# Seven block products of eight for the convolution's second-half projections in a hybrid gated block

## What is computed

```python
proj = jnp.einsum('bld,dn->bln', u, w_in)
(c_b, c_c, c_x, c_z, q, k, v, r, lr_f, lr_b, m_a, m_b) = jnp.split(proj, split_idx, axis=-1)
y_conv = c_b * short_conv_centred(c_c * c_x, conv_w) * jax.nn.silu(c_z)      # 3 taps
p_conv = jnp.einsum('blc,cd->bld', y_conv, w_out_c)
# ... gated linear attention in two directions gives o ...
p_gla = jnp.einsum('blc,cd->bld', rms_norm(o, gla_g) * jax.nn.silu(r), w_out_g)
merged = jax.nn.sigmoid(m_a) * p_conv + jax.nn.sigmoid(m_b) * p_gla
out = jnp.einsum('bld,de->ble', merged, w_out)
return h + rms_norm(out, g_post)
```

## Time and profile before

| | |
|---|---|
| median of 3 runs | 2919.62 us (2919.02 to 2920.57) |
| profiled execution | 2921.19 us |
| its span on the slowest core (core 3) | 2919.6 us |
| spans of the 8 cores | 2909.6 to 2919.6 us |
| granted clock of TensorE, mean of a core | 0.995 to 0.997 |
| PE busy | 2851.8 us, 98% |
| DVE, ACT, POOL busy | 1815.4, 1381.3, 831.7 us |

### The profile page before, as it was taken

One profiled execution on the slowest core, in us unless ns is written; L12 is line 12 of the kernel. 1 busy time (PEld: TensorE's weight loads), 2 busy tenths in 40 slices (PEclk: granted clock), 3 DMA queues, 4 the chain that ended last, 5 costly groups with the idle time before them and its releaser, 6 DMA issues.

```text
span 2919.6 us, 53947 instructions; the slowest of 8 cores (2909.6 to 2919.6 us)
## 1 busy us (share of the span) xinstructions
PE 2851.8 (98%) x16092; PEld 1468.0 (50%) x16092; DVE 1815.4 (62%) x2786; ACT 1381.3 (47%) x2567; POOL 831.7 (28%) x1278
## 2 busy tenths in 40 slices
PE   6999999999999999999999999999999999999998
PEld 3565644444456554444456555444445655544443
...
GB/s 183 134 140 116 125 101 183 232 173 113 197 106 77 75 84 115 110 232 127 111 216 81 75 68 89 123 142 230 97 152 170 78 72 71 84 137 127 118 112 140
DMA packets 340764, 373.44 MB, mean 128 GB/s; under 512 B 208112, under 2 KB 218352, under 8 KB 339968
## 3 DMA queue, kind: packets, MB, share of 16 engines
...
## 4 chain that ended last, share of the span: by engine, by line
PE 94%; DMA 2%; DVE 1%; issue 1%; POOL 1%; ACT 0%; SPq 0%; DVEq 0%; POOLq 0%; ACTq 0%
PE ps L479 94%; DMA sb_onT<-x 0%; DMA sb_onT<-sb_ON 0%; DMA wsc<-sb_W 0%; DMA sb_W<-w_all 0%; DMA sb_KT<-sb_GR 0%; POOL sb_stat L674 0%; PE ps L484 0%; POOL sb_SB L514 0%; DMA sb_ycT<-x 0%; DVE sb_CS L509 0%; DVE sb_ycT L505 0%; DVE sb_TB L509 0%; POOL sb_stat L514 0%; DVE sb_CS L505 0%
## 5 line engine op out<-in xcount | busy, mean ns | idle before, releaser
L479 PE MATMUL ps<-sb_uT,sb_W 128*128 128x512 bf16 (+2 forms) x7840 | 1625.9, 366 | 1.9 <-DMA sb_W<-w_all 1.2
L479 PEld LDWEIGHTS ps<-sb_uT,sb_W 128*128 128x128 bf16 (+1 forms) x7840 | 707.8, 98 | 808.9 <-issue 20.4
L496 ACT ACTIVATE sb_CS<-ps 128x512 f32<-128x512 f32 (+2 forms) x528 | 281.2, 540 | 636.2 <-PE ps L479 605.2
L505 DVE TENSOR_TENSOR sb_CS<-ps,sb_CS 128x512 f32<-128x512 f32 (+1 forms) x408 | 281.0, 691 | 187.9 <-PE ps L479 177.6
L509 DVE SCALAR_TENSOR_TENSOR sb_CS<-sb_CS,ps 128x512 f32<-128x512 f32 x256 | 175.8, 687 | 295.6 <-PE ps L479 284.3
L505 POOL TENSOR_TENSOR sb_GR<-sb_CS 128x512 bf16<-128x512 f32 x128 | 162.1, 1267 | 671.0 <-DVE sb_CS L509 658.5
L479 PE MATMUL ps<-sb_GR 128*128 128x512 bf16 (+2 forms) x1792 | 347.5, 318 | 1.1 <-POOL sb_GR L505 1.1
L505 POOL TENSOR_TENSOR sb_CS<-sb_CS 128x512 f32<-128x512 f32 x128 | 164.8, 1291 | 276.7 <-DVE sb_CS L509 168.6
L479 PE MATMUL ps<-sb_V,sb_uT 128*128 128x256 bf16 x2048 | 239.3, 274 | 0.0
L479 PE MATMUL ps<-sb_onT,sb_W 128*128 128x512 bf16 x1024 | 232.2, 379 | 2.6 <-DVE sb_onT L509 2.6
L509 DVE SCALAR_TENSOR_TENSOR sb_CS<-sb_CS,sb_convw 128x512 f32<-128x512 bf16 x256 | 209.8, 832 | 39.8 <-ACT sb_CS L496 27.6
...
## 6 DMA issues: line engine op xcount, KB each, us to landing
sb_W<-wsc SPq DMA_DIRECT2D x440, 256.0 KB, 2.6
sb_onT<-x SPq DMA_DIRECT2D x56, 512.0 KB, 5.4
sb_W<-wst SPq DMA_DIRECT2D x112, 256.0 KB, 2.8
sb_W<-w_all POOLq DMA_DIRECT2D x80, 256.0 KB, 6.2
sb_GR<-x SPq DMA_DIRECT2D x40, 512.0 KB, 5.5
wsc<-sb_W SPq DMA_DIRECT2D x80, 256.0 KB, 4.4
y<-sb_GR SPq DMA_DIRECT2D x32, 512.0 KB, 3.4
sb_ycT<-x SPq DMA_DIRECT2D x32, 512.0 KB, 5.4
```

The costliest lines, as they stand in the source:

```text
L479: S.add("pe", lambda e: e.matmul(out, lhsT=lhsT, rhs=rhs, start=start, stop=stop, skip_group_check=more), r, w, cost=max(0.025, free_n(rhs ...
L496: S.add("act", lambda e: e.activation(out=out, in_=in_, func=func, **kw), r, w, table=TABLE.get(func), cost=0.17 + 0.82e-3 * free_n(in_) + ...
L505: S.add(eng, lambda e: e.tensor_tensor(out=out, in0=a, in1=b, op=op), r, w, cost=ecost(eng, free_n(out), narrow(out, a, b)))
```

## The change

The convolution stage computes its four projections for each j as two groups of seven products, `(cc, cx)` and `(z, cb)`, in a new function `conv7`. `Seven` is rewritten: the result of p1 is copied by ACT, p6 is followed by a DVE sum that is written back into its PSUM bank, on which p7 and p4 then go on summing, and ACT copies that bank and p5's. The last product p4 of a group is put into the next group, after that one's p6; an output tile follows it in two of three groups. Weight sums for all 16 pairs of the convolution are made in batch 0, in the first half's blocks (`own`), where the weights are held until both of a pair are there. In the gate stages p7 and p4 move apart, with output projections between. Scratch regions `SB`, `SM`, `ON` become one region `OS` that also holds `Seven`'s copies. The next batch's token loads 2 to 7 (and 8 to 11 behind them) may be emitted only after the gate unit mb of block i - 2 of the second half; before, only the end of the first gates and the reuse of their four buffers held them. The diff, cut to its core:

```diff
-    wst_d = nc.dram_tensor("wst", [8 * 128 * 8, 256], BF16, kind="Internal").ap()
+    wst_d = nc.dram_tensor("wst", [24 * 128 * 8, 256], BF16, kind="Internal").ap()
...
+        def npk():
+            best = None
+            for i in range(8):
+                if i in G["held"]:
+                    continue
+                k = ("ps", i)
+                t = max([S.free["pe"]] + [S.last_w[k].end if k in S.last_w else 0.0] + [r.end for r in S.readers.get(k, ())])
+                t -= 0.0 if (i ^ 1) not in G["held"] else 0.4
+                if best is None or t < best[0]:
+                    best = (t, i)
+            if best is None:
+                raise NotReady()
+            i = best[1]
+            G["held"] = G["held"] + (i,)
+            return psb[i], [("ps", i)]
...
-        sd1, sd2, sd5 = (Buf("CS", 8192 + z * 2048, 2048) for z in range(3))
+        sdA = [Buf("CS", 8192 + z * 2048, 2048) for z in range(3)]
+        def sdL(dt):
+            return lrT[:, :].bitcast(dt), [("lr", 0), ("lr", 1)]
+        sdB = [Buf("OS", z * 2048, 2048) for z in range(3)]
+        sdC = [sdB[0], sdB[1], sdL]
+        wtmp = {"m": [Buf("CS", 8192, 2048), Buf("CS", 10240, 2048)], "c": [Buf("onT", 28 * KB + z * 2048, 2048) for z in range(2)]}
...
+        class Seven:
...
+            def __init__(self, pair, X, Y, t0, sd, done, total):
+                self.t0, self.sd, self.done, self.total = t0, sd, done, total
+                self.h = [w2.reserve(X), w2.reserve(("S", pair, 0)), w2.reserve(("S", pair, 1)), w2.reserve(("Y", Y))]
+                self.bk = {}
...
+            def keep(self, bk, z):
+                o_ap, o_k = self.sd[z](F32)
+                act(o_ap, bk[0][:, 0:512], AF.Copy, bk[1], o_k)
+            def bank(self, name, new=False):
+                if new:
+                    G["s7", self, name] = npk()
+                return G["s7", self, name]
+            def p1(self):
+                a = self.bank("a", True)
+                self.mul(a, 0, 0, self.u(0, 0), True)
+                self.keep(a, 0)
+            def p5(self):
+                e = self.bank("e", True)
+                self.mul(e, 1, 0, self.tt(0), True)
+                self.keep(e, 2)
+            def p6(self):
+                b_ = self.bank("b", True)
+                self.mul(b_, 1, 512, self.tt(1), True)
+                s_ap, s_k = self.sd[0](F32)
+                tt("dve", b_[0][:, 0:512], b_[0][:, 0:512], s_ap, ALU.add, b_[1] + s_k, b_[1])
+                self.keep(b_, 1)
+                rel(self.h[1])
+            def p2(self):
+                a = self.bank("a")
+                self.mul(a, 0, 512, self.u(4, 0), False)
+                rel(self.h[0])
+                self.done(0, 0, a)
+            def p3(self):
+                e = self.bank("e")
+                self.mul(e, 2, 0, self.u(4, 512), False)
+                self.total(0, e, self.sd[1])
+                drop(e[1])
+            def p7(self):
+                b_ = self.bank("b")
+                self.mul(b_, 2, 512, self.tt(2), False)
+                rel(self.h[2])
+                self.total(1, b_, self.sd[2])
+            def p4(self):
+                b_ = self.bank("b")
+                self.mul(b_, 3, 0, self.tt(3), False)
+                rel(self.h[3])
+                self.done(1, 0, b_)
...
+                    if own:
+                        sums_w(hs["cc"], hs["cx"], 8 + j, wtmp["c"])
+                        rel(hs["cc"])
...
+        def conv7(b, j):
...
+            def done1(f, s, bk):
+                if f == 0:
+                    o_ap, o_k = ccb[0](F32)
+                    act(o_ap, bk[0][:, 0:512], AF.Copy, bk[1], o_k)
+                else:
+                    times(pv(BF16, 1, 512), (bk[0][:, 0:512], bk[1]), ccb[0](F32), "dve")
+                drop(bk[1])
+            def total1(f, bk, part):
+                dst = ccb[1] if f == 0 else part
+                d, p_ = dst(F32), part(F32)
+                tt("dve", d[0], bk[0][:, 0:512], p_[0], ALU.add, bk[1] + p_[1], d[1])
+                if f == 1:
+                    times(pv(BF16, 513, 512), d, ccb[1](F32))
+            def done2(f, s, bk):
+                if f == 0:
+                    z_ap, z_k = szb[0](BF16)
+                    act(z_ap, bk[0][:, 0:512], AF.Silu, bk[1], z_k)
+                    drop(bk[1])
+                else:
+                    G["cb", me] = bk
+            def total2(f, bk, part):
+                d, p_ = part(F32), part(F32)
+                tt("dve", d[0], bk[0][:, 0:512], p_[0], ALU.add, bk[1] + p_[1], d[1])
+                if f == 0:
+                    z_ap, z_k = szb[1](BF16)
+                    act(z_ap, d[0], AF.Silu, d[1], z_k)
...
+            def cb(s):
+                out = ycT(1, j)(BF16, s * 512, 512)
+                if s:
+                    times(out, sdC[2](F32), tcb[1](F32))
+                else:
+                    bk = G.pop(("cb", me))
+                    times(out, (bk[0][:, 0:512], bk[1]), tcb[0](F32), "dve")
+                    drop(bk[1])
...
+            put("C", lambda: cb(1), ("cb", me, 1), [("sv", b, 1, j, "z", "p7")])
+            put("C", lambda: cb(0), ("cb", me, 0), [("sv", b, 1, j, "z", "p4")])
+            g1 = Seven(8 + j, ("cc", j), ("cx", j), 1024, sdB, done1, total1)
+            g2 = Seven(16 + j, ("z", j), ("cb", j), 1024, sdC, done2, total2)
+            u1 = g1.units((b, 1, j, "c"), {"p4": ("cx", me, 1)})
+            u2 = g2.units((b, 1, j, "z"), {"p2": ("z", me, 0), "p3": ("z", me, 1)})
+            if j > 2:
+                last = (b, 1, j - 1)
+                for p, a in (("p2", ("zm", last, 0)), ("p3", ("zm", last, 1)), ("p5", ("cb", last, 1))):
+                    u2[p][2].append(a)
+            return u1, u2
...
-                    sv = Seven((b, hh, d), d, ("ma", d), ("mb", d), t0, fin)
-                    for p, fn, ti in (("p1", sv.p1, None), ("p5", sv.p5, 0), ("p6", sv.p6, 1), ("p2", sv.p2, None), ("p3", sv.p3, None),
-                                      ("p7", sv.p7, 2), ("p4", sv.p4, 3)):
-                        units[p] = (fn, ("mb", b, hh, d, 1) if p == "p4" else ("sv", b, hh, d, p),
-                                    [("TT", b, hh, ti)] if ti is not None else [])
+                    sv = Seven(d, ("ma", d), ("mb", d), t0, sdB if hh else sdA, done, total)
+                    units.update(sv.units((b, hh, d), {"p4": ("mb", b, hh, d, 1)}))
+                    if hh and d == 0:
+                        units["p1"][2].extend([("cb", (b, 1, 7), 0), ("cb", (b, 1, 7), 1)])
                 ho = {n: w1.reserve((n, d)) for n in ("oc", "og")}
...
-                    order = ["p1", "p5", "p6", "p2", "p3", "p7", ("oc", 0), "p4", ("oc", 1), ("og", 0), ("og", 1)]
+                    order = ["p1", "p5", "p6", "p2", "p3", ("oc", 0), "p7", ("oc", 1), "p4", ("og", 0), ("og", 1)]
...
-                    a.append(("og", b - 1, 0, 7, 1))
+                    a.append(("mb", b - 1, 1, i - 2, 1) if 2 <= i < 8 else ("og", b - 1, 0, 7, 1))
...
+            pend = None
+            n = 0
-                ca, cz, cbb, _ = conv_units(b, 1, j)
-                units = ca + cz + cbb
-                for n, (fn, name, aft) in enumerate(units):
-                    if n % 4 == 0 and t7:
+                for g in conv7(b, j):
+                    for p in ("p1", "p5", "p6"):
+                        put("D2", *g[p])
+                    if pend is not None:
+                        put("D2", *pend["p4"])
+                    if n % 3 < 2 and t7:
                         put("D2", *t7.pop(0))
-                    put("D2", fn, name, aft)
+                    for p in ("p2", "p3", "p7"):
+                        put("D2", *g[p])
+                    pend = g
+                    n += 1
+            if t7:
+                put("D2", *t7.pop(0))
+            put("D2", *pend["p4"])
```

183 lines of the change are left out of this document (89 added, 94 removed).

## The result

The changed kernel takes 3026.11 us (median; the kernel before 2920.1 us in the same session): 1.036 times as long, 95% interval 1.034 to 1.038. The prediction was 2900 us with a range of 2880 to 2936 us: a gain was forecast, and the kernel became slower, by 90 us beyond the upper end of the range. The profiled execution took 3026.24 us with a span of 3024.7 us.

The account below looks back on a forecast made before the run. PE was taken as the bound, busy 2851.8 of 2919.6 us. Terms -41.4 - 2 + 17.6 + 4 + 2 = -19.8 us took 2921.19 to 2901.4, less 1.57 to 2899.8, stated as 2900 us, range 2880 to 2936.

Parts of the forecast that it names:

- What goes: Convolution stage: 192 matmuls fewer at 215.8 ns each, a gain of 41.4 us.
- pace: Rival: a removed matmul gives back only 118 ns, 22.6 us for the 192, ending at 2919 us; chance 0.03.
- Where cover is thin: Four convolution groups per batch without an output tile lose 1.1 us each through late VectorE or weights, 17.6 us.
- covered: Rival: loads stand ahead of stores and VectorE keeps up, leaving exit and 1 us of batch 0: 2881 us; chance 0.14.
- The price of a tap: VectorE in the convolution stage: each of four taps per channel block priced at 0.89 us.
- (b): Groups without a tile: weight load fits by 0.3 to 0.6 us; behind store and residual load PE waits 1.4 us.
- (a): p7 after p6 in groups without a tile: 0.7 us spare; a scale or two taps ahead cost 0.6 to 1.1 us.
- slower rival: Store and residual load precede weights in each thin group, VectorE's queue costs 0.9 us in all sixteen: 2936 us; chance 0.26.
- A wait on a free bank: Sign against the forecast: PE waiting on a free PSUM bank would show it wrong.
- Batch 0: First phase: weight sums for 16 pairs, 32 stores and longer-held buffers cost 2 us, bounds 0 and 18 us.
- The gate stages: Output projections between p3, p7 and p4 take back 2 us of PE's waits on VectorE sums (0 to 2.9).
- Exit: Last convolution group: p4 directly behind p7 with a VectorE sum between, 1.0 us per batch, 4 us.

Follow-up runs that it names:

- e12: Changed kernel with seven products only for (cc, cx), both z products ahead of p7, batch 0's second half as before, first-half residual sums on VectorE: ratio 0.9983 to kernel before.
- e5: Changed kernel with the residual sum of the first half's output tiles made by VectorE, never POOL: ratio 1.0245 to the kernel before.
- e11: e5 plus an output tile in each of the first eight groups, so groups without one come last: two runs, 2982.8 and 2988.5 us.
- e7: Changed kernel with the output tiles' stores issued from POOL's queue instead of SP's: ratio 1.0441 to the kernel before.
- e1: Changed kernel without the weight sums of batch 0's convolution pairs, their stores and the longer-held buffers: ratio 1.0279 to the kernel before.
- e13: Changed kernel with batch 0's 64 VectorE sums made from token tiles, not stored, no buffer held: ratio 1.0292 to the kernel before.
- e15: e11 with batch 0's second half as before the change, making the sums of its twelve pairs there: ratio 1.0051 to the kernel before.
- e2: Changed kernel with the old convolution stage and no convolution weight sums in batch 0: ratio 1.0003 to the kernel before.
- e4: Changed kernel with the next batch's token loads back in the convolution stage: ratio 1.0471 to the kernel before.

## Why the prediction was wrong

**What goes** was right: 24 matmuls less are 5.18 us less where nothing waits (e12), 215.8 ns each. The rival "pace" is out, and so is the 131 ns that the prediction cited from the Trainium skill: by it the 24 would have been worth 3.1 us. VectorE's total was right as well, 76.5 us busy in the stage of batch 1 against 78: what failed is not its load but its order.

**Where cover is thin** is the step that failed. It looked for the thin place between p6 and p7 in the four groups without a tile. The long waits stand at p4, eight of fifteen of them in groups that have a tile: p4 of the second pair is put behind p1, p5 and p6 of the next group and ahead of its tile, 12 matmuls behind p7, so the tile that was counted as cover comes after it. The prediction saw the sum between p7 and p4 only at the end of the stage (1.0 us; measured 0.9). Behind those 2.59 us of cover VectorE has the sum of p3, a scale, two taps and its own sum: 0.69 + 1.27 + 1.66 + 0.68 = 4.3 us even at 0.83 us a tap. The wait on this was 40.7 us in 19 places; four of these, 3.8 us, are the exit, and the other 37 us had no term. The rival "covered" rested on a row read too widely: the 2.9 us of the earlier trace rows are PE's waits on VectorE's sums alone; the same view of the kernel before has 30 us more on other tiles of VectorE, 24 of them in the first 30 us of the span.

**The price of a tap** was mis-sized with it: 0.89 us from the trace of before, 1.26 in the mean here and up to 2.65 beside POOL's residual sum. The 0.89 was a mean already: 0.75 us for a tap with no POOL instruction beside it, and 1.39 to 1.49 for one that starts beside a POOL product. The residual sum was VectorE's in the earlier trace rows; the planner gives it to whichever engine is free first by its model, and here that was POOL for half of the tiles. The prediction took over the durations of before without asking which work the planner would move. e5 shows the price of it, together with the order that came of the move: 30 to 40 us.

**The weights** (b) were right in mechanism and about in size: 21.2 us in the convolution stages against 17.6 us for (a) and (b) together; the longest 4.3 us against a bound of 3.2. Of the 21.2 us 17.7 stand at the first or second product behind a group without a tile, 1.1 us for each of the 16 such groups. A store and a residual load stand ahead in the timeline shown (5.0 us to landing, 4.6 in the earlier trace rows). In the changed kernel no weight load landed before a store, a residual or a token load that was issued ahead of it and still under way (232 pairs). e11, which takes store and load away from most of these groups, leaves 4.4 us; e7 shows that SP's order alone is not it. (a), at p7, was about the 4.2 us of waits on ScalarE's copies. The slower rival named this mechanism and would have decided from 2.3 us a thin group on; the weights cost 1.1 to 1.3 us a thin group. The kernel came out slower, beyond that rival's 2936 us, for another reason than the rival's.

**The clock** had no term: the earlier trace rows shows 1.00 in these stages, and the prediction did not ask what waits of over 2 us do to it. 44.4 us at 0.5 are 22 us lost in the convolution stages, and 24 us more of them in batch 0 and the first gates are 12 us. The stages add up: 400.4 us of matmuls, 72 us of waits that have a row, 22 us of clock, 494 of 506.3. Most of the other 12 can be estimated: a matmul lasts 379 ns but follows the one before after 215.8, so that where PE runs dry another 0.16 us is lost that no view counts as a wait; 51 waits make 8 us, and gaps too short for the view (under 0.15 us) add 2.

**A wait on a free bank** was listed as what would be wrong, and it is there: 0.15 us ahead of p1, four times in batch 1, and once 0.3 us (the last two lines of its waits), small.

**Batch 0** was put at 2 us, "near the lower end, since in that phase other matmuls can go ahead"; the bounds were 0 to 18. It cost 26 to 27 us (e1). The idle of an engine over a whole phase says little of an order that is full at single points: e13 gives 11 us for VectorE's operations alone, and the hold, priced at nothing, costs 16 by itself. About 10 us of the 26 are clock: 37.5 us of that part are at the lower level, 17.1 before. In e15 the same kind of sums does not lengthen the convolution stage of batch 0, and costs some 5 us behind it.

**The gate stages** were to gain 2 us. With the old convolution stage the new order shows no gain (e2, 417.2 us); behind the new one the second gates are 9 us longer, the work that the convolution leaves on VectorE and ScalarE at their start being part of it (the first p7 of batch 1 waits 1.0 us, and all waits there make 2.7 of 3.3 us). The token loads, priced at nothing there, cost the second gates nothing: with the loads early (e4) these last 421.6 us as well. That the move was needed was right.

**Exit** was 4 us and is: the last p4 waits 0.9 us in batch 1.

The large errors have one direction: the price of a step was read from a kernel in which PE had not to wait for that engine, and the cover was taken from a stage and not from the twelve matmuls in question.
